# SyncE's order at the change from the first feed-forward matrix to the second: two weight blocks and a token load ahead of a store

## What is computed

```
h = rmsnorm(x, norm_ffn)
x = x + square(relu(h @ w_ffn1)) @ w_ffn2        # w_ffn1: 1024 x 4096, w_ffn2: 4096 x 1024, float32
y = rmsnorm(x, norm_final)
```

## Time and profile before

| | us |
|---|---|
| median of three runs | 1682.06 |
| lowest and highest | 1680.97, 1682.78 |
| the profiled execution | 1680.67 |
| its span, first to last instruction | 1678.7 |
| TensorE busy in it | 1630.2 (97%) |
| VectorE busy | 1165.1 (69%) |
| ScalarE busy | 805.2 (48%) |

### The profile page before, as it was taken

The page is one execution under the profiler, slowest core; times in us unless marked ns, Lnnn a source line. Parts: engine busy times, 40 slices in busy tenths (PEclk is TensorE's granted clock), DMA queues, the critical chain, the costliest instruction groups (busy, mean ns, idle before and its releaser), DMA issues.

```text
span 1678.7 us, 26263 instructions
## 1 busy us (share of the span) xinstructions
PE 1630.2 (97%) x10302; PEld 1452.0 (86%) x10302; DVE 1165.1 (69%) x1762; ACT 805.2 (48%) x1301; POOL 37.6 (2%) x49
## 2 busy tenths in 40 slices
PE   9999999999999989999999999999999999999998
PEld 8877777888999977888988889999999888888886
DVE  7477777666868688556165786666666787777786
ACT  5577777774535367314274533333332343433344
POOL 1000000000000002001000100000000000000001
PEclk9999999999999999999999999999999999999999
DMA  6221322211102252720272224333444863444332
GB/s 205 77 81 55 86 71 61 68 38 40 38 28 67 65 170 78 269 63 26 76 203 72 104 82 145 131 121 127 145 145 164 328 214 122 141 144 155 126 101 113
DMA packets 157691, 190.72 MB, mean 114 GB/s; under 512 B 5505, under 2 KB 117761, under 8 KB 155522
## 3 DMA queue, kind: packets, MB, share of 16 engines
q1 hardware_dynamic: 157570, 189.05, 34.5%
HBM read 134.84 MB, written 54.20 MB: 113 GB/s over the span
## 4 chain that ended last, share of the span: by engine, by line
PE 48%; DVE 3%; issue 1%; ACT 1%; POOL 0%; DVEq 0%; POOLq 0%; ACTq 0%
PE PS L2863 7%; PE PS L2865 7%; PE PS L2864 7%; PE PS L2684 7%; PE PS L2680 7%; PE PS L2682 6%; PE PS L2006 1%; PE PS L2004 1%; PE PS L2005 1%; PE PS L591 1%; PE PS L2106 1%; PE PS L2547 1%; PE PS L2549 1%; PE PS L2548 1%; DVE sbuf_ops_S L2534 0%
## 5 line engine op out<-in xcount | busy, mean ns | idle before, releaser
L629 PE MATMUL PS<-sbuf_h_hi,sbuf_w_hi 128*128 128x384 f32 x600 | 211.4, 352 | 1.2 <-ACT sbuf_g_N L645 1.2
L631 PE MATMUL PS<-sbuf_h_hi,sbuf_w_lo 128*128 128x384 f32 x600 | 201.8, 336 | 0.0
L630 PE MATMUL PS<-sbuf_h_lo,sbuf_w_hi 128*128 128x384 f32 x600 | 201.5, 336 | 0.0
L2863 PE MATMUL PS<-sbuf_ops_w,sbuf_go_u 128*128 128x512 f32 x448 | 174.6, 390 | 2.3 <-DVE sbuf_gg_X L2952 2.3
L2864 PE MATMUL PS<-sbuf_ops_w,sbuf_go_u 128*128 128x512 f32 x448 | 174.3, 389 | 0.0
L2865 PE MATMUL PS<-sbuf_ops_w,sbuf_go_u 128*128 128x512 f32 x448 | 174.3, 389 | 0.0
L2680 PE MATMUL PS<-sbuf_ops_S,sbuf_ops_w 128*128 128x288 f32 x512 | 150.8, 295 | 2.4 <-DVE sbuf_ops_S L2534 1.3
L2684 PE MATMUL PS<-sbuf_ops_S,sbuf_ops_w 128*128 128x288 f32 x512 | 151.1, 295 | 0.0
L2682 PE MATMUL PS<-sbuf_ops_S,sbuf_ops_w 128*128 128x288 f32 x512 | 150.8, 294 | 0.0
L2705 ACT ACTIVATE sbuf_ff_u<-PS 128x576 f32<-128x576 f32 x64 | 41.5, 649 | 168.5 <-DMA uD<-sbuf_ff_sums 97.1
L629 PEld LDWEIGHTS PS<-sbuf_h_hi,sbuf_w_hi 128*128 128x128 f32 x600 | 113.2, 189 | 9.8 <-issue 7.8
(11 more groups left out here) (335 smaller groups left out, 3800.7 us busy)
## 6 DMA issues: line engine op xcount, KB each, us to landing
sbuf_gg_u<-uD SPq DMA_DIRECT2D x28, 1024.0 KB, 5.1
uD<-sbuf_ff_u SPq DMA_DIRECT2D x16, 1152.0 KB, 4.2
sbuf_ff_raw<-w_ffn SPq DMA_DIRECT2D x16, 1024.0 KB, 6.9
sbuf_gg_B<-w_ffn SPq DMA_DIRECT2D x16, 1024.0 KB, 8.1
sbuf_raw<-w_in SPq DMA_DIRECT2D x28, 512.0 KB, 4.6
uD<-sbuf_ff_sums SPq DMA_DIRECT2D x16, 768.0 KB, 6.2
sbuf_X<-x_prompt SPq DMA_DIRECT2D x16, 512.0 KB, 7.3
xD<-sbuf_X SPq DMA_DIRECT2D x9, 512.0 KB, 2.6
```

The costliest lines, as they stand in the source:

```text
L629: pe.matmul(out, hi, h_hi[:, kb, tok], start=kb == 0, stop=False)
L630: pe.matmul(out, hi, h_lo[:, kb, tok], start=False, stop=False)
L631: last = pe.matmul(out, lo, h_hi[:, kb, tok], start=False, stop=kb == KB - 1)
L2863: pe.matmul(out, u_hi, x_hi, start=first, stop=False, skip_group_check=True)
```

## The change

One line moves. SyncE issues the store of unit 14 after the loads of B12 and B22 and no longer before them; the wait that B22 has of its own now also stands ahead of the store.

```
             block_unit("B21", 0)
             sp.wait_ge(f_p, FF_AT["P7", LASTU] + 1)
             u_unit(1)
-            store_u(LASTU - 1)
             block_unit("B12", 0)
             sp.wait_ge(f_p, FF_AT["P5", LASTU] + 1)
             block_unit("B22", 0)
+            store_u(LASTU - 1)
             u_unit(2)
             for t in (4, 5, 6, 7):
                 stream_back(t)
```

## The result

Over 19 executions of each kernel in turn, the median went from 1681.0 to 1683.74 us. The ratio is 1.0014, with a 95% interval of 1.0008 to 1.0021: by it the changed kernel is slower by 2.4 us (1.3 to 3.5); the two medians themselves differ by 2.7 us. That is what was forecast, less than 0.2% and on the slower side.

A forecast was written before the change was run, and what follows sets the result against it. TensorE was taken to set the end behind its wait near 1340; the median of 1682.06 us plus VectorE's delay of 1.96 us, arriving once, gave 1684.0 us, range 1681.8 to 1686.2.

The forecast's parts named there:

- What bounds: Behind the wait near 1340, TensorE sets the end; a microsecond lost or gained there arrives at the end as one.
- The numbers: Whole kernel: 1684.0 us, 1.2 to 2.8 us slower (chance 0.74); within 0.2% 0.84, there on the slower side.
- The queue in order of issue, and the store's place: DMA queue: transfers land in order of issue; B12 and B22 4.7 us sooner, the sums' store 5.3 us later.
- Rival A: DMA queue: the store is not held up by the loads, TensorE's 2.26 us wait goes, 1679.6 us; chance 0.05.
- The loads are early to no use: Ahead of T3 on VectorE: B12 and B22 will have been there for 6.8 us, to no use.
- VectorE 1.96 us late, T3 on: VectorE: T3 starts at 1330.77 against 1328.81, and 1.96 us can't be made up before add(1, 0).
- On TensorE once, and not twice: TensorE, product k = 1: new 1.9 us wait for u piece 7, old 2.26 us wait stays; sum + 1.96 us.
- rival C: TensorE behind its two waits: the granted clock falls, costing 1.7 us more, 1685.7 us; chance 0.09.
- Rival B: DMA queue: bytes mix, the store lands half way, T3 starts within 0.3 us of 1328.81, 1682.1 us; chance 0.07.
- Rival D: SyncE or ScalarE: a later wait taken for slack costs another 1 to 3 us, up to 1687; chance 0.05.

The follow-up runs named there:

- after_again: The changed kernel, unaltered, run again for a second profile: 1683.66 us, ratio 1.0014 against the kernel before (1681.24 us in the same session).

## Why the prediction was right

*What bounds.* Right. Nothing behind 1345 absorbed anything; from tile 2 to the end of the span it takes 336.8 us before (1678.7 - 1341.90) and 336.9 in after_again.

*The numbers.* The ratio is what was forecast, but two of the absolute times agree better than they have a right to. The forecast of 1684.0 us (measured 1683.74) started from a median of three executions, 1682.06, and the median of 19 is 1681.0; from there + 1.96 makes 1683.0. And T3 at 1330.77 (measured 1330.73) and the sums' store at 1328.7 (measured 1328.7) came out by luck: in this profile u_unit(1) was issued 1.07 us later than before, and the queue was 1.2 us less behind. ScalarE's idle time, 6.63 us where 7.7 was forecast, shows the second of these.

*The queue in order of issue, and the store's place.* Right. I had the sums' store 5.3 us later. Counted from the landing of u_unit(1), ScalarE starts u piece 4 at 12.63 - 7.9 = 4.7 us before (first profile) and at 16.87 - 6.7 = 10.2 after: 5.4 us later. Rival A needed a store that overtakes loads; none did in any of the profiles, so it falls, and the ratio of 1.0014 is on its other side. In all 13 profiles the six transfers from u_unit(1) to u_unit(2) landed in the order in which they were issued. The single steps are less even than the forecast took them: the u store and the sums' store took 2.4 and 2.3 us in the first profile before, and 3.1 and 1.6 in the first one after. Their sum stayed at 4.7.

The Trainium skill (page "DMA: Bandwidth & Descriptors", section "HWDGE ordering") says that completion is not in order for the issuing engine as a whole. For these transfers of 0.75 to 1.1 MB one behind the other, no run here shows that. I had read the section too widely: it also says that the write which raises a transfer's semaphore lands only after every earlier write of the same DMA engine, and its own example has a transfer on one DMA engine behind one on 16. With loads and stores that all use the same DMA engines it would give the order of issue, and the trace agrees.

*The loads are early to no use.* Right: T3 started 6.7 us after B22 had landed, 6.8 was forecast.

*VectorE 1.96 us late, T3 on.* Right in size, 2.0 us, by the table. By the plain difference of the first two profiles it would look wrong (0.85), and by the means counted from the issue it is 1.7.

*On TensorE once, and not twice.* Right in kind: a new wait for u piece 7 and the old one unchanged, 2.26 and 2.24 us. The new wait was mis-sized against the first profile of before: 0.73 to 0.87 us in the three profiles after, not 1.9. It was reckoned from a base that already held the slow queue: in the first profile before, piece 7 came 0.14 us before its matmul and so was just in time, 25.2 us from u_unit(1). Where the queue is less far behind (second and fourth profile before) T3 is 0.9 to 1.3 us sooner, piece 7 with it, so the new wait has that slack to use up first, and in exchange the old wait there was 1.4 and 1.1 us, not 2.26. The two changes add up to the same 2 us: 0.8 + 2.2 after against 1.1 (fourth profile before), 1.9 in all.

*The rest of the 2.4 us.* 2.0 are delay, some 0.2 the clock (rival C, as a small share of executions and not as the rule; not clear of nothing), and the remaining 0.2 are inside the interval. Rival B falls by the last column of the table: T3 did not stay. Rival D needed a further wait of TensorE; after 1345 there is none.

## What to carry to other kernels

When a transfer is moved back in a saturated queue, look for who waits for it because of its *buffer*, not only for its data: what unit 14's store writes is read by nobody here before the last turn's first load of it, issued at 1534.4, and yet it frees the place that the next stage writes. Loads put ahead of it pay only when the engine that wants them reaches them before it reaches the instructions that wait for the store; the order of the queue and the order of that engine have to be changed together (1.0014 and 1.0017 apart, 0.9978 together). And when two profiles are subtracted for a microsecond, take the times from an event inside the resource in question: counted from the landing of an unmoved transfer, T3 agreed to 0.1 us in six profiles; from its issue it spread by 1.3.

## What was unexpected about the hardware

The backlog of one and the same queue, with the same transfers issued at the same distances, differed by 1.3 us between profiles of one kernel (u_unit(1) landed 6.6 to 7.9 us after its issue), while T3 followed that landing by the same 10.1 us in all four. The steps in between were not all the same: the u store landed 2.2 to 3.0 us behind u_unit(1) and the sums' store 1.7 to 2.5 behind it, but 4.7 together.

The granted clock fell to 0.50 for 3.4 us behind tile 2's wait in some executions of both kernels and not in others, with nearly the same idle time in front: 0.73 and 2.24 us in the first profile after (it fell), 0.87 and 2.25 in the second (it did not); 2.24 in the third profile before (it fell), 2.26 in the first (it did not). A fall costs 1.4 us, more than half of what this change costs, and comes on top as noise.
